# A ten-mixer transformer stack on one core: the last gate blocks of two layers, their value matmuls and the weight splits are placed differently

## The chip, the core and the metric

The kernel runs on one core of a Trainium2 chip. The core's engines are TensorE (PE in the profile; its weight loads are PEld), VectorE (DVE), ScalarE (ACT), GpSimd (POOL) and SyncE (SP); each works through a queue of its own in order, and they wait for each other by semaphores. The metric is device time of one execution in microseconds (us). Three runs of the kernel before are shown: 2591.42, 2593.69 and 2613.07, median 2593.69.

## The reference, cut to what matters

512 tokens of width 1024, all in float32, pass through two stacks. The first has four layers: MLA, SWA (a sliding window), NSA, MLA; each is

```
shift, scale, gate = split(silu(c) @ ada_w[i] + ada_b[i], 3)
h = rmsnorm(x, norm_g[i]) * (1 + scale) + shift
x = x + gate * mixer(h)

swa: q, k, v, g = split(h @ w_in);  q, k = rope(q), rope(k)
     o = softmax over a band of keys, with a sink per head (16 heads, 2 key heads, d = 64)
     return (o * silu(g)) @ w_out
nsa: the same with three branches: compressed keys, selected blocks, a window;
     o = g0*o_c + g1*o_s + g2*o_w;  return (o * silu(g)) @ w_out
```

The second stack has two layers with four mixers each: retention, differential attention, SSD and mLSTM. All attention is causal.

## The kernel before, in words

Activations are kept transposed: a "block" is 128 features by 512 tokens. Every large product is made in three matmuls of split operands (`product`, L514: high x high, high x low, low x high), 128x128 weights against 512 columns. So each 1024x256 unit of weights must be split: DVE copies it rounded into a high part (`part_high`, L1560) and subtracts it for the low part (`part_low`, L1566; in `split` the same at L1537 and L1538). SP loads the units into three slots of `wring`, one after the other; a load waits until the unit three before it is used up. There are two slots for high parts, so a split waits for the unit two before it.

The silu gate of a layer has four such units, ("gate", 0) to ("gate", 3), each two blocks of 8 chunks by 3 matmuls. ACT copies a finished block from PSUM and writes its tanh into one of the two slots `th` (that is `pr[:, 2:4]`); DVE multiplies (`gate`). In the same DVE loop stand `ada_rows`: steps of the next layers' `silu(c) @ ada_w`, 16 per modulation part, whose weights POOL loads (512 KB each, at most two ahead; POOL waits for DVE's rows before it issues the next). PE sums them in `modulation`, 16 one-column matmuls at L613.

Attention (`attention` on PE, ACT and DVE, `normalise` on POOL) goes over steps: one pair of heads by one tile of 128 queries, i.e. 16 steps in MLA and in the later differential attention, 32 in SWA, 64 in NSA. A step: PE scores (L643; in SWA first the sink columns, L636), DVE masks and takes the row max (L1639), ACT exponentiates and sums (L1218), DVE inverts the sum (L1643), POOL scales (L2326), PE transposes (L657) into one of two banks, DVE or ACT copies (L1662, L1665, L1230, L1233), PE multiplies with the values (L822 in SWA, L914 in NSA). Scores run two steps ahead of the transposes, values one behind. The probabilities of step m stand in slot m mod 4 (`rows_slot`); slot 1 is `pr[:, 2:4]`, so ACT's first exp waits for the last gate. When a pair of heads is done, DVE takes it through three stages (`out_unit`: multiply with the gate, high part, low part), one per step. At steps 5 and 9 DVE writes a whole high part of the next weight unit, at steps 7 and 11 its low part. The output projection follows.

What is ahead of the first step: in SWA the four gate units, two modulations and their waits. In NSA also the compressed branch: its scores for four query tiles (L857) lie after gate units 0 (two tiles), 1 and 2; DVE and ACT make a softmax of each, POOL multiplies twice per tile (L2342, L2344; in POOL's queue behind its ada loads), PE transposes after the modulations (L891) and DVE copies (L1960). PSUM: four banks for scores (0 to 3; 0 to 2 are the ring A of the gates, 3 to 5 the ring V), two for transposes (4, 5), two for outputs (6, 7: ring O).

## Time and profile before

| | |
|---|---|
| median of 3 runs | 2593.69 us |
| the profiled execution: time, span | 2609.59 us, 2607.7 us |
| busy: PE, PEld, DVE, ACT, POOL | 91%, 69%, 60%, 29%, 18% |
| mean granted TensorE clock | 0.936 of full |
| chain that ended last | PE 70%, DVE 16%, ACT 5%, issue 3%, DMA 3%, POOL 2% |
| from first to last attention matmul: SWA | 435.2 to 544.7 us |
| the same: NSA | 831.9 to about 993 us |

The page gives busy time per engine, the span in 40 equal slices, the chain of waits that ended last, and groups of instructions. The trace can be asked for stretches ("windows"), for the instructions of one engine in order of time ("timeline"), for waits and for the chain.
### The profile page before, as it was taken

Reading aid. Unit: us, or ns where it says so; the run is one execution under the profiler, and the core shown is the slowest. Engines: PE = TensorE matmul, PEld = TensorE weight load, DVE = VectorE, ACT = ScalarE, POOL = GpSimd, SP = SyncE. Lnnn points to the kernel's source line nnn. Section 1 sums busy time; section 2 is a strip of 40 time slices with the busy share of each in tenths; the row PEclk is TensorE's granted clock in tenths of the full one; section 3 lists DMA queues with packets and bytes.
Section 4 is the critical chain, followed back from the end, with each engine's and each line's share of the span. In section 5 each row is a group of like instructions: output and inputs, shape, how many; then the busy total and the mean of one; then the engine's idle time right before and its main releaser. Section 6 shows DMA issues by size and latency. Waiting matters only on the chain.

```text
span 2607.7 us, 30434 instructions
## 1 busy us (share of the span) xinstructions
PE 2373.2 (91%) x11909; PEld 1790.4 (69%) x11909; DVE 1561.3 (60%) x2556; ACT 754.0 (29%) x1638; POOL 456.6 (18%) x624
## 2 busy tenths in 40 slices
PE   3989899998998999899699989999889998999987
PEld 2767677776776667677577856586667786658666
DVE  7566674564276766557645478664744546866473
ACT  2343212313102561433312152323310225232321
POOL 1212212311013551202100012200320001220030
PEclk6999898588998999999799999999999999999999
DMA  6540465032474004240122211122122221112111
GB/s 222 153 129 8 122 146 130 1 113 81 89 157 102 2 2 113 82 121 1 65 65 65 81 33 49 49 81 65 55 75 81 65 66 33 49 49 81 56 58 64
DMA packets 222544, 199.49 MB, mean 77 GB/s; under 512 B 85859, under 2 KB 205507, under 8 KB 222147
## 3 DMA queue, kind: packets, MB, share of 16 engines
q1 hardware_dynamic: 210883, 155.60, 20.9%
q0 software_dynamic: 11520, 41.95, 5.4%
q8 instruction: 96, 1.57, 0.3%
q14 instruction: 45, 0.37, 0.0%
HBM read 194.39 MB, written 2.10 MB: 75 GB/s over the span
## 4 chain that ended last, share of the span: by engine, by line
PE 70%; DVE 16%; ACT 5%; issue 3%; DMA 3%; POOL 2%; SPq 0%; DVEq 0%; ACTq 0%; POOLq 0%
PE bank L517 15%; PE bank L518 15%; PE bank L519 15%; PE bank L643 5%; PE bank L657 3%; PE bank L679 3%; DMA mix<-in_ada_w 2%; DVE wring_parts L1538 2%; PE bank L593 2%; DVE whi_parts L1537 2%; DVE mix L1727 1%; DVE qb L2060 1%; PE bank L791 1%; DVE bank L1639 1%; PE bank L537 1%
## 5 line engine op out<-in xcount | busy, mean ns | idle before, releaser
L518 PE MATMUL bank<-h_parts,whi_parts 128*128 128x512 f32 (+2 forms) x1248 | 496.9, 398 | 0.0
L1538 DVE TENSOR_TENSOR wring_parts<-wring,whi_parts 128x2048 fp32r<-128x2048 f32 (+1 forms) x126 | 283.6, 2251 | 4.3
L518 PEld LDWEIGHTS bank<-h_parts,whi_parts 128*128 128x128 f32 (+2 forms) x1248 | 231.7, 186 | 64.0 <-issue 5.9
L1537 DVE CAST whi_parts<-wring 128x2048 fp32r<-128x2048 f32 (+1 forms) x126 | 150.7, 1196 | 175.6 <-PE bank L519 142.9
L518 PE MATMUL bank<-mix_parts,whi_parts 128*128 128x512 f32 x512 | 204.5, 399 | 0.0
L517 PE MATMUL bank<-vt_parts,whi_parts 128*128 128x512 f32 (+2 forms) x456 | 191.9, 421 | 5.9 <-DVE wring_parts L1538 5.9
L519 PE MATMUL bank<-vt_parts,wring_parts 128*128 128x512 f32 (+2 forms) x456 | 182.2, 400 | 0.0
L643 PE MATMUL bank<-kb,qb 64*128 64x128 f32 (+3 forms) x1024 | 160.1, 393 | 6.2 <-ACT pr L1175 2.7
L1639 DVE CUSTOM_DVE_ANT_0 bank<-bank,causal 128x256 f32<-128x256 f32 (+3 forms) x256 | 120.5, 513 | 70.8 <-PE bank L643 70.3
L517 PE MATMUL bank<-pt_parts,whi_parts 128*128 128x512 f32 x368 | 151.7, 412 | 10.5 <-ACT kb L1150 5.3
L517 PE MATMUL bank<-mix_parts,whi_parts 128*128 128x512 f32 (+1 forms) x392 | 155.2, 396 | 0.0
L519 PE MATMUL bank<-mix_parts,wring_parts 128*128 128x512 f32 (+1 forms) x392 | 155.0, 396 | 0.0
L2307 POOL DMA_DIRECT2D mix<-in_ada_w x80 | 64.6, 808 | 505.9 <-DVE mix L1727 493.9
L519 PE MATMUL bank<-pt_parts,wring_parts 128*128 128x512 f32 x368 | 146.0, 397 | 0.0
L519 PE MATMUL bank<-whi_parts,h_parts 128*128 128x256 f32 (+1 forms) x480 | 134.0, 279 | 0.0
L643 PEld LDWEIGHTS bank<-kb,qb 64*128 64x128 f32 (+1 forms) x1024 | 102.8, 221 | 33.4 <-issue 18.6
L1727 DVE SCALAR_TENSOR_TENSOR mix<-mix,cond 128x512 f32<-128x512 f32 x140 | 105.2, 752 | 30.4 <-DMA mix<-in_ada_w 26.2
L1606 DVE SCALAR_TENSOR_TENSOR tmp<-bank,st 128x512 f32<-128x512 f32 x55 | 38.0, 692 | 126.6 <-PE bank L593 123.7
L518 PEld LDWEIGHTS bank<-mix_parts,whi_parts 128*128 128x128 f32 x512 | 97.7, 191 | 23.4 <-issue 1.0
L1218 ACT ACTIVATE pr<-bank,stat 128x128 f32<-128x128 f32 (+4 forms) x160 | 72.8, 460 | 133.4 <-DVE stat L1639 102.4
L517 PEld LDWEIGHTS bank<-vt_parts,whi_parts 128*128 128x128 f32 (+2 forms) x456 | 84.8, 186 | 38.0 <-issue 9.2
L517 PE MATMUL bank<-kb_parts,whi_parts 128*128 128x512 f32 x224 | 91.2, 407 | 16.1 <-POOL mix_parts L2370 11.5
(406 smaller groups left out, 5047.8 us busy)
## 6 DMA issues: line engine op xcount, KB each, us to landing
wring<-in_w_in SPq DMA_DIRECT2D x60, 1024.0 KB, 5.2
mix<-in_ada_w POOLq DMA_DIRECT2D x80, 512.0 KB, 4.6
wring<-in_w_out SPq DMA_DIRECT2D x16, 1024.0 KB, 5.3
wring<-in_mla_w_in SPq DMA_DIRECT2D x10, 1024.0 KB, 5.5
wring<-in_mla_w_out SPq DMA_DIRECT2D x8, 1024.0 KB, 5.3
wring<-in_swa_w_in SPq DMA_DIRECT2D x32, 256.0 KB, 4.7
wring<-in_nsa_w_in SPq DMA_DIRECT2D x32, 256.0 KB, 4.5
wring<-in_nsa_w_in SPq DMA_DIRECT2D x6, 1024.0 KB, 5.1
```

The lines of the kernel that those rows point to most:

```text
L517: pe.matmul(bank, lh, rh, start=start, stop=False)
L518: pe.matmul(bank, lh, rl, start=False, stop=False)
L519: return pe.matmul(bank, ll, rh, start=False, stop=stop)
L643: mm = pe.matmul(b[s][:, lo:hi], q[:, i * P:(i + 1) * P], k[:, first + lo:first + hi], start=(c == 0), stop=(c == len(terms) - 1 and (c == ...
L657: mm = pe.transpose(turn_bank(n)[:, at * P:(at + 1) * P], rows_slot(m, s)[:, c * P:(c + 1) * P], ident[:, :])
L679: mm = pe.matmul(bank[:, j * P:], v(j), pt[:, u % 2, j, j * P:], start=(j == 0 and not opened), stop=(j == NT - 1 and last))
L1218: act.activation(rows_slot(m, s)[:, 0:wide], bank[:, 0:wide], ACT.Exp, scale=-1.0, bias=stat_at(0, m, s), accum_out=stat_at(1, m, s)).then ...
L1537: chain(dve.tensor_copy(high, whole))
L1538: dve.tensor_tensor(low, whole, high.bitcast(F32), ALU.subtract).then_inc(done, 1)
L1639: dve.tensor_tensor_reduce(bank, bank, mask, -1.0, least, ALU.add, ALU.min, stat_at(0, m, s)).then_inc(max_ready, 1)
L1727: dve.scalar_tensor_tensor(out=to, in0=t, scalar=cond[:, k:k + 1], in1=to, op0=ALU.mult, op1=ALU.add).then_inc(ada_step, 1)
L2307: pool.dma_start(ada_ring[:, u % 2, :].rearrange("p (k n) -> p k n", k=2), w[:, k:k + 2, c:c + S]).then_inc(ada_loaded[u % 2], 16)
```

## The change

- SWA and NSA: gate unit 3 is not made ahead of attention. `late_gates` on PE makes its two blocks, both at once over the 8 chunks, in four pieces of 12 matmuls: two pieces after score 0, one after score 1, one after the first transposes. They go to ring O. The modulations, and in NSA the transposes of the compressed branch, come after the first two pieces, inside the attention. ACT copies the two blocks and takes the tanh into `vt[:, 0:2, 512:]` after its step 0; DVE multiplies them at steps 2 and 3. DVE's part of the modulations (in NSA also the copies of the transposes) comes after row max 0.
- SWA and NSA: values run two steps behind the transposes; DVE's stages of a finished pair come one step later.
- The `ada_rows` of the eight gates are spread over six: 3, 3, 3, 3, 2, 2.
- NSA: compressed scores of tiles 2 and 3 both follow gate unit 1.
- All six attentions: the weight splits at steps 5 to 11 become pieces, one a step from step 3 to 14: two high pieces of 1024 columns and four low ones of 512 for each of two units.
- `rows_slot`: the slot that shares memory with `th` is now that of step 3, and in SWA and NSA ACT waits for the last early gate before its exps of step 3.

The diff, cut where lines repeat what is said above:

```diff
-PREPARE_AT = (5, 9)
+PREPARE_FROM = 3
 AHEAD = 2
+LATE_VALUES = (1, 2)
 LOW_LAG = 2
...
-NSA_SCORES = ((0, 1), (2,), (3,))
+NSA_SCORES = ((0, 1), (2, 3), ())
...
-            return (pr[:, 0, :], pr[:, 1, :], pr[:, 2, :], pr[:, 3, :], raw[:, 0, 4:], raw[:, 1, 4:], rs[:, :], tmp[:, :])[2 * (m % 4) + s]
+            return (pr[:, 0, :], pr[:, 1, :], raw[:, 0, 4:], raw[:, 1, 4:], rs[:, :], tmp[:, :], pr[:, 2, :], pr[:, 3, :])[2 * (m % 4) + s]
...
+            def late_gates(L):
+
+                slots = by_chunk(weights(L, ("gate", 3)))
+                b = [open_bank(O, (L, "gate", 6 + j)) for j in range(2)]
+                for k in range(KC):
+                    for j in range(2):
+                        mm = product(b[j][:, :], [t[:, k, j * P:(j + 1) * P] for t in slots], hk(k), k == 0, k == KC - 1)
+                        if k == KC - 1:
+                            mm.then_inc(O.full, 1)
+                    if k == KC - 1:
+                        used(O.filled((L, "gate", 7)))
+                    if k % 2:
+                        yield
+
             def in_tokens(L, name, ring, key, n, at=0, slots=None):
...
-            def attention(L, scores, values):
+            def attention(L, scores, values, fill=None):
 
                 todo = steps(L)
+                behind = 2 if L in LATE_VALUES else 1
 
                 def score(m):
...
                     score(m)
+                    if fill:
+                        fill(m)
                 for m in range(len(todo)):
                     if m + AHEAD < len(todo):
                         score(m + AHEAD)
                     turn(m)
-                    if m:
-                        value(m - 1)
-                value(len(todo) - 1)
+                    if fill and m == 0:
+                        fill(AHEAD)
+                    if m >= behind:
+                        value(m - behind)
+                for m in range(len(todo) - behind, len(todo)):
+                    value(m)
...
                     rope_swap((L, "k", 0))
-                    for i in range(4):
+                    for i in range(3):
                         in_blocks(L, ("gate", i), A, [(L, "gate", 2 * i + j) for j in range(2)])
-                    modulations(L)
                     pe.wait_ge(*cnt(rope_done, 9))
-                    pe.wait_ge(*A.emptied((L, "gate", KC - 1)))
-                    pe.wait_ge(*V.emptied(last_modulation(L)))
+                    pe.wait_ge(*A.emptied((L, "gate", 5)))
+                    late = late_gates(L)
+
+                    def fill(at):
+                        next(late)
+                        if at == 0:
+                            next(late)
+                            modulations(L)
+                            pe.wait_ge(*V.emptied(last_modulation(L)))
...
                             mm.then_inc(V.full, 1)
-                    for i in range(4):
+                    for i in range(3):
...
-                        if i < 3:
-                            for t in NSA_SCORES[i]:
-                                compressed_scores(t)
-                    modulations(L)
-                    for i in range(NT):
-                        pe.wait_ge(*cnt(cmp_pool))
-                        bank = open_bank(V, (L, "tc", i))
-                        for g in range(4):
-                            mm = pe.transpose(bank[:, g * P:(g + 1) * P], pc[:, i, g * P:(g + 1) * P], ident[:, :])
-                        mm.then_inc(V.full, 1)
-                    pe.wait_ge(*V.emptied((L, "tc", NT - 1)))
-
-                    pe.wait_ge(*A.emptied((L, "gate", KC - 1)))
+                        for t in NSA_SCORES[i]:
+                            compressed_scores(t)
+                    pe.wait_ge(*A.emptied((L, "gate", 5)))
+                    late = late_gates(L)
+
+                    def fill(at):
+                        next(late)
+                        if at == 0:
+                            next(late)
+                            modulations(L)
+                            for i in range(NT):
+                                pe.wait_ge(*cnt(cmp_pool))
+                                bank = open_bank(V, (L, "tc", i))
+                                for g in range(4):
+                                    mm = pe.transpose(bank[:, g * P:(g + 1) * P], pc[:, i, g * P:(g + 1) * P], ident[:, :])
+                                mm.then_inc(V.full, 1)
...
+            def late_gates(L):
+                for b in range(6, KC):
+                    act.wait_ge(*O.filled((L, "gate", b)))
+                    bank = O.tile((L, "gate", b))
+                    act.activation(mix[:, b, :], bank[:, :], ACT.Copy)
+                    act.activation(vt[:, b - 6, S:], bank[:, :], ACT.Tanh, scale=0.5).then_inc(O.empty, 1)
+
             def attention(L):
                 todo = steps(L)
-                act.wait_ge(*th_read[-1])
+                if L not in (1, 2):
+                    act.wait_ge(*th_read[-1])
 
                 def exps(m):
                     u, i = todo[m]
...
                     exps(m)
                 for m in range(len(todo)):
                     if m + AHEAD < len(todo):
+                        if m == 1 and L in (1, 2):
+                            act.wait_ge(*th_read[-1])
                         exps(m + AHEAD)
                     keep_turned(m)
+                    if m == 0 and L in (1, 2):
+                        late_gates(L)
 
...
+                (_, name), _, part = unit
+                if part is whole:
+                    return lambda slot: slot[:, first:first + n]
+                return lambda slot: part(slot)[:, first // UNIT:(first + n) // UNIT, :]
+
             def part_low(whole, low, high, done):
 
                 dve.wait_ge(*cut[0])
...
 
             prepared = [0]
 
-            def prepare_high():
+            def prepare_piece(piece):
 
                 s = prepared[0]
                 n = split_units[s]
-                dve.wait_ge(w_loaded[n % W_SLOTS], landed[n])
-                if s >= HI_SLOTS:
-                    dve.wait_ge(*unit_done[split_units[s - HI_SLOTS]])
-                part = units[n][2]
-                part_high(part(W[n % W_SLOTS]), part(W_HIGH[s % HI_SLOTS]))
-
-            def prepare_low():
-
-                s = prepared[0]
-                prepared[0] += 1
-                n = split_units[s]
-                part = units[n][2]
-                part_low(part(W[n % W_SLOTS]), part(W_LOW[n % W_SLOTS]), part(W_HIGH[s % HI_SLOTS]), w_split)
+                whole, low, high = W[n % W_SLOTS], W_LOW[n % W_SLOTS], W_HIGH[s % HI_SLOTS]
+                if piece == 0:
+                    dve.wait_ge(w_loaded[n % W_SLOTS], landed[n])
+                    if s >= HI_SLOTS:
+                        dve.wait_ge(*unit_done[split_units[s - HI_SLOTS]])
+                if piece < 2:
+                    part = columns_of(units[n], 1024 * piece, 1024)
+                    part_high(part(whole), part(high))
+                else:
+                    part = columns_of(units[n], 512 * (piece - 2), 512)
+                    dve.wait_ge(*cut[0])
+                    got = dve.tensor_tensor(part(low), part(whole), part(high).bitcast(F32), ALU.subtract)
+                    if piece == 5:
+                        got.then_inc(w_split, 1)
...
-            def attention(L, out_unit):
+            def late_gate(L, b):
+
+                dve.wait_ge(*O.emptied((L, "gate", b)))
+                O.take((L, "gate", b))
+                dve.scalar_tensor_tensor(out=mix[:, b, :], in0=vt[:, b - 6, S:], scalar=1.0, in1=mix[:, b, :],
+                                         op0=ALU.add, op1=ALU.mult).then_inc(late_gated, 1)
...
+                outs = [(u, stage) for u in range(pairs(L)) for stage in range(3)]
                 for m in range(AHEAD):
                     row_max(m)
-                row_sum(0)
+                    if m == 0:
+                        if early:
+                            early()
+                            row_sum(0)
+                if not early:
+                    row_sum(0)
                 if L >= 4:
...
                     keep_turned(m)
-                    stage = m % NT - (0 if L in (0, 3) else 1)
-                    if u and 0 <= stage < 3:
-                        out_unit(u - 1, stage)
-                    if m in PREPARE_AT:
-                        prepare_high()
-                    if m - 2 in PREPARE_AT:
-                        prepare_low()
-                for stage in range(3):
-                    out_unit(pairs(L) - 1, stage)
+                    if early and m in (2, 3):
+                        late_gate(L, 4 + m)
+                    since = m - (0 if L in (0, 3) else 1) - (1 if L in LATE_VALUES else 0)
+                    if since >= NT and since % NT < 3:
+                        out_unit(*outs.pop(0))
+                    if 0 <= m - PREPARE_FROM < 12:
+                        prepare_piece((m - PREPARE_FROM) % 6)
+                for unit_stage in outs:
+                    out_unit(*unit_stage)
 
             def residual(L, b):
...
+                    for b in range(6):
                         gate((L, "gate", b), mix[:, b, :])
-                        ada_rows(2)
+                        ada_rows(3 if b < 4 else 2)
                         if b in (1, 3):
...
-                    for i in range(4):
+                    for i in range(3):
                         for j in range(2):
                             gate((L, "gate", 2 * i + j), mix[:, 2 * i + j, :])
-                            ada_rows(2)
+                            ada_rows(2 if i == 2 else 3)
                         if i < 2:
                             prepare()
                         if i:
                             for t in NSA_SCORES[i - 1]:
                                 compressed_factors(t)
-                        if i < 3:
-                            for t in NSA_SCORES[i]:
-                                compressed_max(t)
-                modulation(L, 2)
-                if L + 1 < len(LAYERS):
-                    modulation(L + 1, 0)
+                        for t in NSA_SCORES[i]:
+                            compressed_max(t)
+
+                def next_modulations():
+                    modulation(L, 2)
+                    if L + 1 < len(LAYERS):
+                        modulation(L + 1, 0)
+                    if L == 2:
+                        for i in range(NT):
+                            dve.wait_ge(*V.filled((L, "tc", i)))
+                            dve.tensor_copy(ex[:, :, i * P:(i + 1) * P], V.take((L, "tc", i))[:, :].rearrange("p (g n) -> p g n", g=4)).then_inc(V.empty, 1)
+
+                if kind == "mla":
+                    next_modulations()
                 if kind == "nsa":
-                    for i in range(NT):
-                        dve.wait_ge(*V.filled((L, "tc", i)))
-                        dve.tensor_copy(ex[:, :, i * P:(i + 1) * P], V.take((L, "tc", i))[:, :].rearrange("p (g n) -> p g n", g=4)).then_inc(V.empty, 1)
...
-                attention(L, out_unit)
+                attention(L, out_unit, next_modulations if kind != "mla" else None)
```

## Rows read from the trace of the kernel before

**Rows 1.** The page: granted TensorE clock in 40 slices, tenths.

```profile
PEclk6999898588998999999799999999999999999999
```

**Rows 2.** Stretches: us, busy PE PEld DVE ACT POOL (instructions), PEclk, DMA share, GB/s.

```profile
433.00:433.50 0.50, 0.50 (x6) 0.50 (x5) 0.00 (x0) 0.00 (x0) 0.17 (x1) 0.79 1.12 188
435.20:544.70 109.50, 109.00 (x688) 80.73 (x688) 57.19 (x201) 38.94 (x144) 33.12 (x64) 0.51 0.03 7
542.00:543.00 1.00, 1.00 (x11) 0.83 (x11) 0.92 (x2) 0.00 (x0) 0.41 (x1) 0.74 0.00 0
```

**Rows 3.** Timeline, PE before SWA attention: start, length, work [idle before <-releaser].

```profile
428.48 1.84 PE L613 MATMUL bank<-ones,mix 128*128 128x1 f32 x16
432.20 2.61 PE L613 MATMUL bank<-ones,mix 128*128 128x1 f32 x16 [1.87 <-DVE mix L1727]
435.22 0.59 PE L636 MATMUL bank<-sink,ones 1*128 1x1 f32 x4 [0.42 <-issue]
```

**Rows 4.** Chain: start, share, line; a gate matmul, then SWA tiles.

```profile
428.17 0.23 PE bank L518
...
451.94 1.16 PE bank L643 x8
...
453.71 1.05 PE bank L822 x8
454.77 0.52 PE bank L636 x4
...
456.44 1.04 PE bank L657 x4
```

**Rows 5.** Chain of work in NSA attention, full clock.

```profile
842.08 0.59 PE bank L914 x8
842.67 0.65 PE bank L643 x8
843.32 1.03 PE bank L657 x8
```

**Rows 6.** Timeline of PE between NSA gates and attention.

```profile
815.78 1.84 PE L613 MATMUL bank<-ones,mix 128*128 128x1 f32 x16
819.50 3.57 PE L613 MATMUL bank<-ones,mix 128*128 128x1 f32 x16 [1.88 <-DVE mix L1727]
...
831.90 1.65 PE L643 MATMUL bank<-kb,qb 64*128 64x128 f32 x12 [0.78 <-DVE ex L1960]
```

**Rows 7.** Timeline of POOL, same stretch.

```profile
819.75 0.72 POOL L2307 DMA_DIRECT2D mix<-in_ada_w  x1 [4.00 <-DVE mix L1727]
...
828.90 1.05 POOL L2344 TENSOR_TENSOR kb<-kb,aux 128x512 f32<-128x512 f32 x1
```

**Rows 8.** Timeline of DVE before SWA attention: last gate block.

```profile
429.88 0.69 DVE L1619 SCALAR_TENSOR_TENSOR mix<-pr,mix 128x512 f32<-128x512 f32 x1 [3.29 <-ACT pr L1175]
```

**Rows 9.** Stretches of differential attention, as Rows 2.

```profile
1495.00:1532.00 37.00, 27.65 (x214) 20.67 (x213) 29.45 (x103) 22.91 (x79) 9.72 (x16) 1.00 0.08 28
2148.00:2156.00 8.00, 7.78 (x43) 5.92 (x41) 3.86 (x15) 4.03 (x13) 1.19 (x3) 0.65 0.00 0
```

**Rows 10.** NSA attention without its first 8 us, as Rows 2.

```profile
840.00:994.00 154.00, 144.71 (x1411) 102.12 (x1408) 105.08 (x375) 90.27 (x291) 79.46 (x122) 1.00 0.01 2
```

**Rows 11.** Chain of work: compressed scores of two query tiles.

```profile
774.50 3.53 PE bank L857 x32
```

**Rows 12.** Timeline of DVE in NSA attention: two low parts.

```profile
853.63 2.29 DVE L1566 TENSOR_TENSOR wring_parts<-wring,whi_parts 128x2048 fp32r<-128x2048 f32 x1
...
864.60 0.69 DVE L1566 TENSOR_TENSOR mix_parts<-mix,qb_parts 128x512 fp32r<-128x512 f32 x1
```

**Rows 13.** Timeline of POOL, same stretch.

```profile
842.87 0.88 POOL L2326 TENSOR_SCALAR pr<-pr,stat,gbr 128x128 f32<-128x128 f32 x2 [0.36 <-DVE stat L1643]
...
853.25 4.07 POOL L2326 TENSOR_SCALAR pr<-pr,stat,gbr 128x128 f32<-128x128 f32 x4
```

**Rows 14.** Waits of PE in NSA attention: total us, times, longest.

```profile
PE bank L657 <- POOL tmp L2326: 6.0, 11, 1.3
```

16 lines of the change are left out of this document (10 added, 6 removed).

## The prediction

> **What bounds the kernel now.** I read the page first. TensorE (PE) is busy for 91% of the span, so a gain must come from PE work that gets shorter or from PE's idle time. The row of granted clocks [rows 1] then shows where PE is slow: most slices have 8 or 9 tenths, one has 5. Stretches of that region (the windows view) show that the clock falls from 2.4 to 1.2 GHz near 433.3 us and comes back near 542.5 us, which is SWA attention from its first matmul to the output projection: 109.5 us at a mean clock of 0.51, PE busy 109.0 of them [rows 2]. There PE waits for nobody; it is at half clock. It went down after a thin stretch: the last dense gate matmul ended near 428.5, then came 16 one-column matmuls (L613), 1.87 us idle, 16 more, and the first scores at 435.22 [rows 3].
>
> Next the price of a tile of 128 queries with two key tiles. In SWA at half clock (chain of waits): sinks 0.52, scores 1.16, transposes 1.04, values 1.05, so 3.77 us [rows 4]. The same matmul shapes in NSA attention at full clock: scores 0.65, values 0.59, four transposes half of 1.03, so 0.52 [rows 5]. The sinks have no row at full clock; half of 0.52 and 0.52 bound them and I take 0.35, since a tiny matmul is more overhead than columns. Warm tile: 2.11 us. A step with one key tile has half of each part but the sinks: 0.88 + 0.35 = 1.23.
>
> The second loss is ahead of NSA attention: last gate matmul near 815.8, first score at 831.90 [rows 6]. In between PE has only 32 one-column matmuls and 16 transposes; it waits for POOL, whose queue holds an ada weight load behind DVE's last ada row (4.00 us) and whose compressed factors come only after it, until 829.95 [rows 7].
>
> **The change part by part.** The sum is made against the profiled execution (span 2607.7 us, 2609.6 with what lies around it); that one is 0.6% above the median of the runs shown, 2593.7, and the difference carries over unchanged.
>
> (1) SWA attention's clock. Gate unit 3 (48 dense matmuls at 0.23 us [rows 4], 11.1 us) leaves the front and comes in four pieces of 12: two after score 0, one after score 1, one after turn 0. The modulations (about 1.84 us each [rows 3]) stand behind the first two pieces. After unit 2 PE waits for its last gate (copy, tanh: 1.2 us or so, since DVE starts behind both at 429.88 [rows 8] where PE ended near 428.6). The thin stretch is then two modulations, a short drain of V and score 1, some 5 us; before it was about as long when the clock fell. So I expect a dip as well, but now 24 dense matmuls follow it, and near 542.5 us the clock came back when only transposes and values were left, without sinks and scores [rows 2]: it does not take much.
>
> Whether it then holds is the whole question. For it: the differential attention, made of the same kind of small matmuls, held 1.00 for 37 us with PE busy only 27.65 of them, 214 matmuls recorded; and its twin in the next layer came back from 1.2 GHz with 43 matmuls in 8 us, inside attention work [rows 9]. SWA at 1.2 GHz put 688 in 109.5 us [rows 2], 6.3 per us, with narrow operands; warm, the same work is passed 1.8 times as fast (3.77 by 2.11). I expect two stable states, and the change puts the stage into the upper one. The Trainium skill, "TensorE: Matmul & The Clock Gate", section "Why this matters for your kernels", says that keeping TensorE busy brings the full clock and that the loss comes from idle gaps. The first half disagrees with the trace here: busy 109.0 of 109.5 us did not bring it [rows 2]; by it SWA would already be warm, parts (3) and (4) alone would be left, and the time would be 2588; the row leaves that no chance. The second half, which no row tests for this stage, would keep the clock up.
>
> Warm PE work: 8 groups of (1.23 + 3 x 2.11) = 60.5 us. DVE is now near: it is busy 57.19 in this stage [rows 2], plus some 1.3 for split pieces and 1.4 for two late gates (0.69 each [rows 8]), so 59.9. Two in-order engines that both need 60 do not overlap perfectly. Were PE as full as in NSA attention (94%, 144.71 of 154 [rows 10]), 64 us; were DVE only as full as in the differential one (29.45 of 37, 80% [rows 9]), 75. PE and DVE lie between, I take 71. Gain 109.5 - 71 = 38.5, between 34 and 45 by these two.
>
> (2) Entry to SWA. Before: unit 2 ended near 428.5 - 11.1 = 417.4, attention began 435.2: 17.8 us. After: wait 1.2, gates 11.1, modulations 3.7, drain 0.5, one piece at half clock + 2.8, and up to 1 where exps(3) stands behind ACT's four late gate activations and POOL and PE wait for it: 20.3. Cost 2.5. Without the dip it gains 0.3; with two pieces slow it costs 5.3. The ada rows now run three per gate over six gates instead of two over eight, so their loads come a third denser. A late row stalls DVE, but 5.5 us of gate matmuls lie between it and the modulation, where before PE stood idle 1.87 [rows 3]; I take 0, and at most those 1.87. The second part of the thin stretch, DVE's first row max, is followed by its wait for the modulations; row_sum 0, row max 1, ACT's exps 1 and POOL queue behind it, and the next piece (2.8 us) hides that.
>
> (3) NSA entry. Scores 2 and 3 follow gate unit 1, so their factors are started before the last gates end; the last ada row falls with gate 5, and so does POOL's queued load. Walking the engines: unit 1 ended near 815.8 less two units (22.2) and two score tiles (half of 3.53 each [rows 11]), so 790.1. Unit 2's second block then needs a bank that is free only after DVE has done a gate, three ada rows, a weight split, two factors and a max, by my estimate 12 us, and ACT its exp: 802.9, which is a new wait of some 3.5 us for PE. That block is 5.6 long, gate 5 ends at 808.5, DVE's last ada row at 811.8; POOL's load (0.72) and four factors took 10.2 from 819.75 [rows 7], so they end at 822 instead of 830. Under them lie score 0, 24 gate matmuls and the modulations. Score 1 starts near 823.3, 6 us ahead with half a gate unit still to be slotted in at latencies that the first tiles have anyway. I get 6 with a warm clock and 2 with a dip, take 4; ends -2 (dip and late ACT) and 8.
>
> (4) Split pieces and later values. A low part over 2048 columns takes 2.29, over 512 it takes 0.69 [rows 12], so four pieces cost 2.8; the high part in halves about 0.2 more. Per split +0.7 of DVE, hidden in MLA and NSA by PE, half exposed in differential attention. For it: while the 2.29 runs, POOL's four normalisations take 4.07 where two took 0.88 [rows 13], and PE waits on POOL's tmp 6.0 us in NSA, 11 times [rows 14]. The Trainium skill, "SBUF — State Buffer", section "SBUF: two separate sides", calls the port pair of VectorE and GpSimd a lock held for a whole instruction; the trace agrees. By that rule a piece blocks at most 0.69 us instead of 2.29, some 1.6 for each of 12 splits where POOL is late. I take 2 in all, -1 to 5. Values two behind remove waits on copies of the turned rows, 0.2 us in NSA; nothing by themselves, and they keep SWA from stalling at full clock. Out stages move one step later; one stage more (0.7) is left behind the loop, under the first chunks of the output projection. The new row slots only free exps(0) to exps(2) from the last tanh: counted in (2).
>
> Sum: 38.5 - 2.5 + 4 + 2 = 42. Profiled 2567.6, median 2551.7; **forecast 2552 us**. Its own range: least 34 - 5.3 - 2 - 1 = 26, most 45 + 0.3 + 8 + 5 = 58, so 2536 to 2568.
>
> **The rivals.** *The clock stays at 1.2 GHz in SWA.* For it: nothing in the stage raised it for 108 us [rows 2], and the thin stretch is not shorter. Against: 24 dense matmuls after it. Then (1) is 0, (2) costs 5 to 6, (3) and (4) give 4 and 2: 2594, within 2586 to 2600. This is also the case in which the change does not do what it could.
>
> *It rises and falls again midway.* One long wait, on split pieces or out stages of a DVE that is 85% full, would be enough, and nothing later brings it back. Each of 32 tiles that stays cold costs about 1.2 us: half of them give 2552 + 20 = 2572; with three quarters cold 2581.
>
> *Slower: NSA attention loses its clock.* Its entry becomes thin (factors, transposes) and is cut by pieces, as SWA's was. The place is PE in the 162 us from 831.9; price: 144.7 us of PE work times 0.79 (3.77 by 2.11) = 114, so 2666 if all of it stays cold, and slower by 1% from 60% on. Against: before, it came back in the first tiles and was 1.00 from 840 us on [rows 10].
>
> *DVE is slower than I think.* With DVE full only 75%, SWA needs 80 us: 2561; inside the forecast's range.
>
> **How the numbers follow.** Forecast (warm SWA) 0.62, midway 0.10, cold 0.22, slower 0.06. A measurement of this kernel tells about 1% (26 us) from no change. Faster by over 1%: nearly all of the first, under half of the second, 0.63. Within 1%: 0.31. Slower: 0.06. The range for 8 in 10: the warm case without its ends (0.58), midway (0.10) and half of the cold one (0.12) give 2537 to 2594.
>
> **What would show it.** Right: in SWA attention PEclk at 1.00, its stage near 71 us, score rows of 0.65 and value rows of 0.59 instead of 1.16 and 1.05; DVE busy about 85%. POOL's factors before 825 in NSA. L1566 low parts of 0.69 only, and the 4.07 of POOL gone. Wrong: a 5 in the clock row at SWA, with PE again busy all the time; or NSA's first 20 us at 0.50.

## The result, and the profile after

Median 2567.30 us (2566.33 to 2568.20, 4 runs) against 2592.62 us before (2591.42 to 2613.07, 4 runs, the three shown and one more beside it). The medians differ by 25.3 us. The ratio is 0.9895, 95% interval 0.9847 to 0.9943; it and the ratios below are those on record, not quotients of the medians. They leave out as slow each run that took over 1.5% longer than the fastest of its kernel: two in e4, and one in each set of the kernel before that stands beside the experiments. The profiled execution of the changed kernel took 2567.36 us (span 2565.4), which is at its median; that of the kernel before, 2609.59. Between the two profiles lie 42.2 us, the sum that was forecast, and between the medians 25.3. Most of this section is about that difference of 17.

The row of granted clocks, to be read beside [rows 1]: the 5 at SWA is gone.

```profile
PEclk7989899989999998999899999999999999999998
```

Stretches of the changed kernel (us, busy PE PEld DVE ACT POOL, PEclk, DMA share, GB/s): SWA from score 1 to the output projection, the same without its dip, and NSA attention from score 1 to its last score. They answer to [rows 2, 10].

```profile
431.46:504.36 72.90, 69.68 (x705) 52.68 (x705) 56.78 (x207) 40.20 (x144) 34.66 (x64) 0.98 0.09 16
436.00:504.36 68.36, 65.14 (x685) 49.01 (x684) 55.64 (x201) 39.17 (x140) 32.70 (x60) 1.00 0.09 17
795.95:945.60 149.65, 144.98 (x1387) 103.41 (x1388) 107.18 (x392) 92.32 (x297) 75.54 (x124) 1.00 0.04 9
```

From 436 us on SWA is at full clock. DVE is busy 55.64 of 68.36 us there, 81%. The timeline of PE on the way in (start, length, work, idle before and releaser) answers to [rows 3]:

```profile
421.18 0.38 PE L652 MATMUL bank<-sink,ones 1*128 1x1 f32 x4 [1.22 <-issue]
...
427.57 3.63 PE L628 MATMUL bank<-ones,mix 128*128 128x1 f32 x32
...
431.46 0.38 PE L652 MATMUL bank<-sink,ones 1*128 1x1 f32 x4 [0.26 <-DVE mod L1770]
...
434.00 0.63 PE L519 MATMUL bank<-h_parts,whi_parts 128*128 128x512 f32 x1
...
442.92 0.49 PE L659 MATMUL bank<-kb,qb 64*128 64x128 f32 x4
...
504.36 0.50 PE L518 MATMUL bank<-qb_parts,whi_parts 128*128 128x512 f32 x1
```

PE waits 1.22 us (the profile says "issue"; by the code it is the last early gate), makes score 0, two pieces and both modulations; then the clock does fall, as a dense matmul of 0.63 us instead of 0.40 at 434.00 shows, and the third piece ends at full clock again. The output projection begins at 504.36, before at 544.7.

The front of NSA, DVE, PE and POOL in one timeline, answers to [rows 6, 7]:

```profile
744.17 1.54 DVE L1793 SCALAR_TENSOR_TENSOR mix<-mix,cond 128x512 f32<-128x512 f32 x2 [2.84 <-DMA mix<-in_ada_w]
...
752.07 0.79 PE L518 MATMUL bank<-pt_parts,whi_parts 128*128 128x512 f32 x1 [4.75 <-ACT kb L1399]
...
773.01 0.50 PE L518 MATMUL bank<-pt_parts,whi_parts 128*128 128x512 f32 x1 [3.72 <-ACT kb L1399]
...
784.19 0.72 POOL L2378 DMA_DIRECT2D mix<-in_ada_w  x1 [4.88 <-DVE mix L1793]
...
793.38 1.05 POOL L2415 TENSOR_TENSOR kb<-kb,aux 128x512 f32<-128x512 f32 x1
...
795.95 0.71 PE L659 MATMUL bank<-kb,qb 64*128 64x128 f32 x8 [0.79 <-DVE ex L2027]
```

PE waits twice for a bank whose compressed scores ACT has not yet exponentiated (L1399). The first time DVE was late because its ada weights were (2.84 us). POOL's four factors still end at 794.4, and score 1 starts at 795.95. The waits of PE in NSA attention are down from those of [rows 14]; the columns are total us, times, longest:

```profile
PE bank L673 <- POOL pr L2397: 4.0, 7, 1.3
PE bank L673 <- DVE pt L1722: 0.5, 1, 0.5
```

Where the 42.2 us between the profiles lie, with two later profiles beside them (us). Each stretch runs from one matmul with the rope's `swap` matrix (`rope_swap`) to another, the same ones in every kernel, so a layer's stretch takes in the norm and the first projections of the next one:

| stretch | before | before, again (e1) | after | after, again (e12) |
|---|---|---|---|---|
| start to the key swap of SWA | 383.2 | 386.1 | 385.6 | 385.0 |
| from there to the first swap of NSA | 261.4 | 234.7 | 221.2 | 218.3 |
| NSA layer, to the first swap of layer 3 | 450.2 | 453.2 | 449.4 | 449.2 |
| MLA layer, to the first swap of the second stack | 214.6 | 214.8 | 211.9 | 214.7 |
| second stack | 1298.3 | 1300.9 | 1297.3 | 1294.7 |

Nearly the whole effect is in the SWA layer: 40.2 of 42.2 us. The NSA layer, for which the forecast had some 5 us, gives 0.8. The other stretches scatter by 3 to 6 us from profile to profile; where it was read, the granted clock goes with it (the MLA layer took 211.9 us at a mean clock of 0.94 and 214.6 to 214.8 at 0.93). And the kernel before is not one kernel in time: its own SWA layer differs by 27 us between two profiles.

### The profile page after: what moved, and what is told of

It reads as the page before. It is cut to its first block, busy times and chain, and to the rows that moved or that the text cites. A ratio compares the mean times of both kernels' runs of the same rounds, so it can differ in the third digit from the quotient of the medians.

```text
span 2565.4 us, 30479 instructions
## 1 busy us (share of the span) xinstructions
PE 2328.1 (91%) x11909; PEld 1759.8 (69%) x11909; DVE 1563.0 (61%) x2604; ACT 753.7 (29%) x1638; POOL 453.4 (18%) x624
## 4 chain that ended last, share of the span: by engine, by line
PE 68%; DVE 17%; ACT 5%; DMA 3%; issue 3%; POOL 3%; SPq 0%; DVEq 0%; ACTq 0%; POOLq 0%
PE bank L518 15%; PE bank L519 15%; PE bank L520 15%; PE bank L659 4%; DMA mix<-in_ada_w 3%; PE bank L700 3%; PE bank L673 2%; DVE wring_parts L1581 2%; PE bank L608 2%; DVE mix L1793 2%; DVE whi_parts L1580 2%; DVE qb L2131 1%; PE bank L812 1%; PE bank L945 1%; DVE bank L1699 1%
## 5 line engine op out<-in xcount | busy, mean ns | idle before, releaser
L518 PE MATMUL bank<-pt_parts,whi_parts 128*128 128x512 f32 x368 | 155.6, 423 | 17.2 <-ACT kb L1399 8.5
L659 PE MATMUL bank<-kb,qb 64*128 64x128 f32 (+3 forms) x1024 | 142.2, 351 | 6.8 <-ACT pr L1206 3.9
L659 PEld LDWEIGHTS bank<-kb,qb 64*128 64x128 f32 (+1 forms) x1024 | 89.7, 189 | 34.0 <-issue 20.4
L518 PE MATMUL bank<-qb_parts,whi_parts 128*128 128x512 f32 x256 | 105.1, 410 | 0.0
```

What stands on the lines that cost most here:

```text
L518: pe.matmul(bank, lh, rh, start=start, stop=False)
L659: mm = pe.matmul(b[s][:, lo:hi], q[:, i * P:(i + 1) * P], k[:, first + lo:first + hi], start=(c == 0), stop=(c == len(terms) - 1 and (c == ...
```

## The experiments

**The spread of before (e1).** The kernel before, unchanged, three rounds.

> The kernel before, unchanged, looked at once more: its profiled execution took 2609.6 us, the other runs shown 2591 to 2594 and 2613. Theory A (the 18 us sit in one stage: in the shorter executions part of SWA attention runs at full clock): a look of about 2592 us shows SWA attention in some 91 us instead of 109.5. Theory B (they sit in many short dips of the clock elsewhere): SWA attention takes 109 us in every look, and the sum of the other stages is 18 us shorter.

2593.5 us median, 2587.4 to 2612.0 in 10 runs; the profiled execution took 2591.5. With the 78 runs made beside the experiments there are 88 of this kernel: 24 lie between 2609 and 2620 us, 64 between 2576 and 2603. The mean granted clock parts them in the same way: 0.931 to 0.937 in the 24 (the profile of before has 0.936), 0.942 to 0.952 in the 64. The stretches of SWA attention in the profile of 2591.5 us:

```profile
438.00:452.00 14.00, 13.61 (x86) 10.46 (x87) 6.12 (x28) 5.18 (x21) 5.03 (x10) 0.50 0.19 47
454.00:464.00 10.00, 9.87 (x110) 7.40 (x110) 8.70 (x26) 4.86 (x18) 3.87 (x8) 1.00 0.01 2
464.00:466.00 2.00, 0.78 (x13) 0.58 (x11) 1.87 (x7) 0.72 (x3) 1.10 (x2) 1.00 0.00 0
468.00:486.00 18.00, 18.00 (x113) 13.50 (x114) 11.71 (x38) 6.22 (x24) 6.15 (x12) 0.50 0.01 1
488.00:514.00 26.00, 26.00 (x288) 19.71 (x290) 20.06 (x80) 15.43 (x58) 13.15 (x26) 1.00 0.01 2
```

The clock fell at 437, came back near 453.8, fell again near 467.7 and came back for good near 487.9. In the profile of before it stayed down until 542.5 [rows 2]. So theory A holds (its SWA attention, scores from 438.1 to 514.4, ends 24.9 us earlier than before's 539.3). What happened just before it fell at 467 is in the timeline of DVE, POOL and PE:

```profile
462.39 2.28 DVE L1566 TENSOR_TENSOR wring_parts<-wring,whi_parts 128x2048 fp32r<-128x2048 f32 x1
...
464.59 0.15 DVE L1643 RECIPROCAL stat<-stat 128x2 f32<-128x2 f32 x1
...
464.84 1.10 POOL L2326 TENSOR_SCALAR pr<-pr,stat,ones 128x256 f32<-128x256 f32 x2 [2.91 <-DVE stat L1643]
...
465.99 0.66 PE L657 MATMUL bank<-ident,pr 128*128 128x128 f32 x4 [1.22 <-POOL pr L2326]
```

DVE's whole low part (2.28 us) holds the reciprocal of the row sum, POOL waits 2.91 us for it, PE 1.22 for POOL; PE was busy 0.78 of 2 us, and the clock fell behind it. That the stall is the cause rests on e3 and e9 below, where the same happens, and on e4; it was not forced by an edit of its own.

**Each part alone (e2, e3, e4).** The kernel before with one part of the change.

```diff
 e2  LATE_VALUES = (1,)   late gates, ada rows, row slots: SWA only; splits whole
 e3  LATE_VALUES = (2,)   the same for NSA only, with its order of scores; splits whole
 e4  -PREPARE_AT = (5, 9)   nothing else
     +PREPARE_FROM = 3
```

> The change in SWA alone: late gate pieces, ada rows in six gates, values two behind, new row slots; NSA and the weight splits as before. Main theory (nearly the whole gain is SWA's clock): SWA attention from its first regular scores to the output projection 73 us at a clock near 1, total 2568 to 2572 us. Rival (the change in NSA and the split pieces carry a third of the gain): 2576 to 2582 us. Rival (the smaller pieces of DVE work are needed for PE to stay at full clock): the clock falls again within SWA, total above 2585.

2572.2 us (2570.7 to 2580.0 in 10 runs), ratio 0.9896 (0.9861 to 0.9930). Its profile (2579.9 us) from 444 us on:

```profile
444.00:501.00 57.00, 53.69 (x584) 40.41 (x582) 49.14 (x176) 33.45 (x125) 30.14 (x54) 1.00 0.10 20
```

SWA is at full clock in spite of whole splits, so the main theory holds, with the median at the upper end of its 2568 to 2572. The four edits within it (pieces, ada rows, later values, row slots) are parted only by e5 and e10; ada rows and row slots have no run of their own.

> The change in NSA alone. From the two profiles: the front of NSA lost 6 us (two waits of 4.75 and 3.72 us for a bank and two dips of the clock), its attention gained 10, so 4 us net: theory: its total is 4 us below the kernel before in the same state, 2588, and SWA attention stays at half clock. Rival (the gain of NSA attention came from split pieces and not from the late values): 0 to +6 us, 2592 to 2598.

2590.6 us (2574.8 to 2612.9), ratio 0.9982 (0.9940 to 1.0024): no difference that can be told from the spread of before. SWA is untouched here, and its profile shows the same fall as e1, behind the same kind of stretch:

```profile
466.00:468.00 2.00, 1.12 (x12) 0.79 (x12) 1.54 (x9) 1.08 (x5) 1.33 (x3) 1.00 0.00 0
470.00:516.00 46.00, 46.00 (x292) 33.97 (x288) 24.89 (x90) 16.74 (x63) 14.46 (x29) 0.50 0.01 1
```

Its NSA attention took 151.8 us (scores from 819.3 to 971.1, 5.6 of gate pieces within) against 153.7 before, but its front lost as much: the NSA layer took 449.6 us against 450.2. The 4 us of my theory are not there.

> The split pieces alone, in all six attentions; gates, values and row slots as before. My prediction had 2 us of gain for it (-1 to 5). Theory: 2590 us, PE waits for POOL in NSA attention down from 5.9 to about 4 us. Rival (the gain in NSA attention is all theirs): 6 us or more, 2586. Rival (more DVE instructions delay it): 2594 or more.

2574.4 us, ratio 0.9897 (0.9864 to 0.9931): 8 of 10 runs between 2569.6 and 2580.3, two at 2611.5 and 2613.7. None of the three expectations had this size. SWA attention in its profile (2569.8 us):

```profile
436.00:452.00 16.00, 15.62 (x100) 11.80 (x100) 7.52 (x33) 6.54 (x26) 5.04 (x11) 0.50 0.20 45
454.00:500.00 46.00, 45.10 (x488) 33.97 (x486) 41.09 (x154) 27.36 (x103) 23.56 (x46) 1.00 0.01 2
```

The entry is cold as before. But once the clock is back, near 452, it stays: DVE is as full, in pieces of 0.7 us, and PE is busy 45.10 of 46 us. NSA attention took 153.7 us, as before, and PE waited 5.3 us in it for POOL, against 5.0 before: the pieces alone give it nothing. What they gave is SWA's clock.

**What decides at the entry (e5, e6, e9).** e5 moves two of the four pieces of the changed kernel; e6 makes the kernel before enter attention straight from dense work; e9 adds dense work to the kernel before.

```diff
 e5   def fill(at):                      (SWA)
-         next(late)
          if at == 0:
-             next(late)
+             for _ in range(4): next(late)
              modulations(L)
 e6   for i in range(4):                 (before, SWA; ada rows 3, 3, 3, 3, 2, 2)
+         if i == 3: modulations(L)
          in_blocks(L, ("gate", i), ...)
-     modulations(L)
 e9  +def dense():                       (before, SWA; after score 1 and after turn 0)
+        for k in range(12): pe.matmul(spare_bank, h_parts[:, k % KC, 0:P], h_parts[:, k % KC, :])
```

> The changed kernel, but in SWA all four pieces of gate unit 3 stand after score 0 and ahead of the modulations, so that nothing dense follows the thin stretch. Theory (the 24 dense matmuls after the modulations are what makes attention start at full clock): SWA starts at 1.2 GHz again; as the split pieces are in, the clock comes back some 17 us later in most runs, as in the run with the pieces alone: 2572 to 2580 us, with single runs at 2600 or more. Rival (the later values or the shorter thin stretch hold the clock up anyway): within 1 us of 2567.

2604.0 us, 2601.5 to 2606.4 in 10 runs, ratio to before 1.0041 (1.0011 to 1.0071). The modulations' stretch, then attention:

```profile
430.00:434.00 4.00, 3.81 (x34) 3.67 (x32) 0.32 (x3) 0.00 (x0) 0.00 (x0) 1.00 0.56 130
436.00:536.00 100.00, 100.00 (x624) 73.98 (x622) 54.59 (x199) 38.22 (x141) 31.17 (x60) 0.50 0.01 3
```

The first half of the theory is shown, and larger than I had it: two pieces, 24 matmuls, stand one place earlier, and the kernel is 37 to 40 us slower than the changed one (2567.3, and 2563.6 in e12). PE is busy 100.00 of 100.00 us at half clock. Its second half fell: in the profile the clock did not come back after 17 us, and the mean clock of all ten runs, 0.935 to 0.938, is that of executions which are cold through SWA.

> The kernel before with one edit, in SWA: the 16 ada rows are spread over the first six gates and the two modulations stand ahead of gate unit 3, so that 48 dense matmuls lie between them and attention. No late gates, values one behind, whole splits. Theory (what counts is to enter attention from dense work): it starts at full clock, total 2570 to 2576 us. Rival (whole splits stall PE at full clock and throw it back, as at 465 us in the repeated look at the kernel before): starts at full clock and falls after step 9: 2582 to 2595. Rival (the wait for the last gate drops the clock by itself): as before, 2594.

2616.8 us, 2588.7 to 2625.0, nine of ten above 2612; ratio 1.0073 (1.0033 to 1.0112). Dense work, the first tiles, the rest:

```profile
430.00:438.00 8.00, 8.00 (x35) 6.48 (x34) 0.69 (x1) 1.09 (x2) 0.00 (x0) 0.98 0.00 0
438.00:444.00 6.00, 3.98 (x38) 2.91 (x36) 2.52 (x12) 2.91 (x10) 0.70 (x2) 1.00 0.58 124
444.00:542.00 98.00, 97.78 (x608) 72.23 (x608) 51.98 (x183) 34.94 (x130) 30.29 (x60) 0.50 0.02 4
```

My theory fell. Attention was entered at full clock from eight dense us, and the clock fell within its first tiles: PE waits 1.22 us for the last gate, 0.65 for the first exp, 0.38 for POOL, and was busy 3.98 of 6 us. The entry has two thin places, the modulations and the latency of the first tiles, and e6 mended one. That mending the other as well would have been enough was not run.

> The kernel before with work added and nothing else: in SWA 12 dense matmuls (128x128 by 512 columns, 2.8 us each dozen) whose result nobody reads stand behind score 1 and 12 more behind the first transposes, where the changed kernel has the last two pieces of its late gates. Theory (what brings and holds the full clock is dense work between the first tiles): SWA attention runs at full clock although 5.6 us of work are added; with whole splits it can fall once midway: median 2575 to 2585 us, none of the runs above 2600. Rival (the pieces help because they take work out of the front, or the later values and row slots do it): the clock stays down as often as before, median 2594 to 2600, single runs near 2618.

2604.2 us (2599.7 to 2615.4), ratio 1.0041 (1.0010 to 1.0071). Four stretches of its profile:

```profile
434.00:442.00 8.00, 7.58 (x39) 6.66 (x39) 1.97 (x11) 1.83 (x8) 0.92 (x3) 0.50 0.64 139
444.00:474.00 30.00, 28.33 (x283) 21.11 (x283) 22.22 (x75) 14.54 (x54) 11.34 (x22) 1.00 0.01 2
474.00:478.00 4.00, 2.79 (x32) 2.07 (x30) 3.26 (x11) 1.02 (x5) 1.53 (x3) 0.97 0.01 2
478.00:534.00 56.00, 56.00 (x348) 41.27 (x350) 27.03 (x105) 20.89 (x77) 18.00 (x36) 0.50 0.00 1
```

The size was missed: I had 2575 to 2585 and no run above 2600, and nine of ten were above. The mechanism is half right. The clock is down at 434 to 442 and comes up inside the first dense dozen, 8 to 10 us earlier than in e1 and e4, where nothing dense stood there; attention then runs at 1.00 for 33 us. At 474 PE stalls beside the second whole split (2.79 of 4 us busy), the clock falls, and stays down for 56 us; beside the first one, at 463, it did not fall. In this profile 5.6 us were added and the clock was won and lost: dense work lifts it, and does not keep it.

**What holds it (e7, e10).** The changed kernel with whole splits; with the values one step behind.

```diff
 e7  -PREPARE_FROM = 3
     +PREPARE_AT = (5, 9)
 e10 -LATE_VALUES = (1, 2)
     +LATE_VALUES = ()
```

> The changed kernel with whole weight splits at steps 5 to 11 again, all else as changed. Theory (pieces matter only where the clock has fallen; with a warm entry they save 1 to 3 us of waits): 2568 to 2571 us. Rival (they carry the gain of NSA attention too): 2574 or more.

2571.0 us, ratio 0.9930 (0.9889 to 0.9971): 8 of 10 runs from 2566.4 to 2575.5, two at 2594.1 and 2595.7. The profile (2570.8 us), SWA and NSA attention:

```profile
436.00:499.50 63.50, 60.23 (x635) 45.51 (x634) 51.68 (x185) 37.02 (x134) 31.04 (x56) 1.00 0.10 18
793.60:945.30 151.70, 146.99 (x1387) 104.75 (x1388) 106.38 (x384) 92.20 (x297) 76.20 (x124) 0.99 0.04 8
```

The eight runs fit the theory within some us. The other two are as slow as before's middle and have no profile of their own; their mean clock was 0.943, against 0.952 to 0.956 in the eight, so they lost clock somewhere. That a whole split threw them back, as in e1 and e9, is likely but not shown. NSA attention costs 2.1 us more than after's 149.65, but not for want of pieces. It was entered at half clock here and at full clock in the changed kernel (this run's row, then after's):

```profile
793.60:797.00 3.40, 3.38 (x13) 2.75 (x14) 1.07 (x6) 1.02 (x4) 1.15 (x3) 0.50 0.00 0
795.95:799.35 3.40, 3.40 (x20) 2.70 (x20) 1.06 (x6) 1.02 (x4) 1.68 (x4) 1.00 0.00 0
```

Over its first 11.4 us the mean clock was 0.83, which costs some 1.9 us, and PE waited for POOL 4.0 us in the stage, in both kernels. So here too the pieces give NSA nothing that can be seen. The entry is cold in e8 as well, with pieces in, and in e3; why, no run shows.

> The changed kernel with the values of SWA and NSA one step behind the transposes, as before, and the out stages back with them. Theory (the later values are worth the short waits on copies): 2568 to 2571 us, SWA at full clock. Rival (they keep SWA from stalling when it is at full clock): runs at 2590 appear.

2571.9 us, 2568.2 to 2573.4 in 9 runs, ratio 0.9914 (0.9886 to 0.9941), no run near 2590. SWA keeps its clock; the cost is in NSA attention, 155.6 us:

```profile
795.10:950.70 155.60, 147.69 (x1403) 104.15 (x1403) 107.24 (x392) 92.34 (x297) 79.76 (x125) 1.00 0.04 8
```

That is 5.95 us more than with later values, out of 8.3 us between its median and e12's. PE waits for POOL 6.3 us in it, against 4.0, and for DVE's copies 1.2 against 0.5. These 3.0 us are half of it; the other half is in no wait, and up to the output projection PE is busy 153.30 us against 151.06 with the same matmuls. It stays unexplained.

**The front of NSA, and a version that beats both (e8, e11, e12).**

```diff
 e8   gate(L, 2 * i + j)
+     if j: compressed_max of the unit's tiles      (was behind rows, split and factors)
-     ada_rows(3, 3, 3, 3, 2, 2)
+     ada_rows(2, 2, 3, 3, 3, 3)
 e11 as e8, and:
+     compressed_factors(0), (1) ahead of the split; (2), (3) ahead of the last rows
+     ada_rows(2, 3, 3, 4, 2, 2)
+     POOL: the four factors ahead of its last two ada loads of the stage
+     PE: late gate piece 0 ahead of score 0, in SWA and NSA
```

> The changed kernel with another order of DVE in the front of NSA: the maxima of the compressed scores come right behind the second gate of the unit, ahead of its ada rows and the weight split, and the ada rows run 2, 2, 3, 3, 3, 3 over the six gates instead of 3, 3, 3, 3, 2, 2. It aims at the two waits of PE for a bank (4.75 and 3.72 us) and the dips of the clock behind them (1.6 to 2.4 us each). Theory: most of it comes back, total 2556 to 2561 us. Rival (DVE is the bound of that stretch, the waits only move): 2564 to 2567. Rival (the last ada row comes later and the modulations wait for it): above 2568.

2563.1 us (2560.8 to 2564.1, 4 runs), ratio 0.9886 (0.9816 to 0.9957). By its total it is not told from the changed kernel, which had 2567.3 and 2563.6 us in its two sets of runs; the profile says more. Both bank waits are gone, and something new is late (DVE, then PE):

```profile
772.79 1.54 DVE L1811 SCALAR_TENSOR_TENSOR mix<-mix,cond 128x512 f32<-128x512 f32 x2 [4.42 <-DMA mix<-in_ada_w]
...
784.88 1.11 PE L929 MATMUL bank<-ident,kb 128*128 128x128 f32 x4 [1.24 <-POOL kb L2440]
...
786.78 1.23 PE L661 MATMUL bank<-kb,qb 64*128 64x128 f32 x8 [0.78 <-DVE ex L2052]
```

The last ada rows waited 4.42 us for their weights, POOL's factors queued behind that load, and PE waited 5.2 us for them in four parts. The waits moved, as the second rival has it, though not all of them. Gates and NSA attention together took 4.8 us less than in the changed kernel (from the last swap matmul, 722.2 to 937.9 against 725.1 to 945.6).

> A version meant to beat both. The changed kernel with three more edits: in the front of NSA DVE takes the maxima of the compressed scores ahead of the ada rows and the factors of tiles 0 and 1 ahead of the weight split, those of 2 and 3 ahead of the last ada rows (rows 2, 3, 3, 4, 2, 2); POOL multiplies the factors ahead of its last two ada loads; in SWA and NSA the first late gate piece stands ahead of score 0 and covers the wait of 1.2 us for the last early gate. Theory: 6 us less than the 2563 us of the version with the maxima first, since PE's 5.2 us of waits for POOL go, and 1 to 2 us for the pieces: 2553 to 2558. Rival (the queue of DVE is full there, the waits move to the gates): 2560 to 2564. Rival (with one piece less between score 0 and the modulations SWA loses its clock): above 2590.

2559.0 us, 2556.4 to 2560.0 in 6 runs, ratio to before 0.9860 (0.9822 to 0.9898). Beside it on the same chip:

> The changed kernel once more, beside the others on one chip. Theory: 2567 us within 2, with none of the spread of the kernel before (2577 to 2620). Rival (its four runs were lucky): single runs above 2580.

2563.6 us, 2563.0 to 2569.2 in 6 runs, ratio 0.9883 (0.9844 to 0.9921). I had 2567 within 2, so two sets of runs of one kernel can lie 3.7 us apart; the small differences of e7 and e8 to the changed kernel, which did not run beside it, are no larger. e11 did run beside it. The two sets do not overlap; e11 is 4.6 us faster than the changed kernel, 1 us short of my range. PE in its NSA front:

```profile
766.87 0.80 PE L520 MATMUL bank<-pt_parts,whi_parts 128*128 128x512 f32 x1 [3.21 <-DVE wring_parts L1592]
...
780.67 3.31 PE L926 MATMUL bank<-ident,kb 128*128 128x128 f32 x16
...
784.85 0.71 PE L661 MATMUL bank<-kb,qb 64*128 64x128 f32 x8 [0.88 <-DVE ex L2048]
```

The transposes of the compressed branch now run without a break, and score 1 starts 63.6 us after the last swap matmul (784.85 against 721.26) where the changed kernel takes 70.8. A wait of 3.21 us for the weight split that was put behind the factors is what it pays. Its SWA layer took 218.2 us, e12's 218.3: the earlier piece gave nothing there.

## Why the prediction was right, and where it was not

**The sum.** The median came out at 2567.3 us where 2552 was forecast, 0.7 us inside the upper end of the range. The direction and the main mechanism were right: SWA attention went from half to full clock. The size at the median was 25.3 us instead of 42. Against the profiled execution the sum was 42 and the profiles differ by 42.2, and that agreement is luck: the terms are off by +4.8, +1.9, -9.9 and +7.7 us, and 4.3 were lost outside them. Term by term, from the profiles:

| step | forecast | measured |
|---|---|---|
| (1) SWA attention's clock | 38.5 (34 to 45) | 43.3 |
| (2) entry to SWA | -2.5 | -0.6 |
| (3) entry to NSA | +4 (-2 to 8) | -5.9 |
| (4) pieces, later values | +2 (-1 to 5) | 9.7 in NSA attention |

(1) and (2): from the end of gate unit 2 to the output projection before took 127.3 us, after 84.6 (419.8 to 504.4). In it are 1.4 for the last gate, 13.2 for 48 gate matmuls and 3.9 for the modulations and their drain, some 18.4 in all; 66.2 us are left for attention. I had 71, because I put PE and DVE halfway between two stages with more waits; the stage is nearer its PE work of 60.5 (DVE is at 81%, forecast about 85). The warm prices were nearly right: scores 0.65, values 0.59, transposes 0.59 (forecast 0.52), sinks 0.31 from start to start (0.35).

(3) has the wrong sign. The new wait in unit 2's second block was forecast at 3.5 us and measured 3.72. The same wait one unit earlier, 4.75 us, was not seen, nor the dips of the clock behind both (0.50 over 752 to 757, 0.66 over 773 to 778, by my estimate 2.5 and 1.7 us). Together they make 9.2 of the 9.9 us. The step that failed is "I take 0" for the denser ada loads: I asked only whether PE's modulation would wait for a late row, and in NSA the compressed maxima stand behind those rows in DVE's queue. e8 bears it out: with the maxima ahead both waits are gone, though it also moved ada rows, so the two were not parted.

(4) The mis-sized term is the later values, "nothing by themselves". By e10 they are worth 5.95 us in NSA attention. I had counted only the waits on copies, and misread those: 0.2 us stands beside POOL's raw, and the row of the copies is

```profile
PE bank L657 <- DVE pt L1662: 1.6, 8, 0.3
```

Nor had I seen that values put between the transposes and the next scores give POOL time (PE's waits for it fall from 6.3 to 4.0 us). Another 3.7 come without them (153.7 against e10's 155.6 less 5.6 of gates), and the clock of the first tiles accounts for it: the first 8 us before ran at 0.50 and 0.57, by my estimate 3.8 us lost, and e10 has 1.00 there. Both together are the 9.7. For the pieces, to which I gave the 2 us, nothing is left in NSA (e4, e7): their low parts take 0.69 us as forecast, and POOL's longest run of four normalisations went from 4.49 to 3.31 us, but PE waits for POOL no less. Their use is in SWA (e4), which the forecast did not have.

The four terms measured add up to 46.5. Of that 2.4 us were lost ahead of SWA, 2.5 between its attention and the first swap of NSA, 1.6 in the projections that open NSA and 1.4 behind its attention, and 3.7 won in layer 3 and the second stack; each is of the size of the scatter in the table.

**The step that failed** is the one ahead of the sum: "the difference carries over unchanged". The profiled execution of before was the case of 24 in 88, cold through the whole of SWA. In the other 64 the higher mean clock, and e1's profile of one of them, say that the clock comes back for a part of it, and those runs had already a good part of the gain. The changed kernel has no such spread (10 runs, 2563.0 to 2569.2). So the change is worth 45 us against the first kind and 25 to 30 at the median. A spread of 22 us in three runs was on the table, and a profile above the median by 16; the 2613.07 among the runs should have been read as a second course of the same program.

**The rivals.** "Midway", which I gave 0.10 for the changed kernel, is what the kernel before does: in e1, in e3 (SWA as before) and in e9 (before with work added) the clock falls behind a stall beside a whole split. Its 2572 us lie nearer to the measured 2567.3 than the forecast's 2552, but the changed kernel did not take that course: its SWA was at 1.00. My clause "nothing later brings it back" fell: it came back after 20 us in e1 and after 48 in e3. "Two stable states" is too strong for the same reason. The cold rival did not come; e5 shows that it hung on where two pieces stand. The slower one, NSA losing its clock, did not come either: its attention was at 1.00.

**The rule.** By the sentence cited from the Trainium skill, "TensorE: Matmul & The Clock Gate", section "Why this matters for your kernels", that a busy TensorE brings the full clock, e5 would have been at full clock after its entry; the rows show 100.00 us busy and 0.50. The half about idle gaps agrees with e1, e6 and e9, and not with e2, where PE stood idle 1.67 of 4 us and the clock stayed. The same page of the Trainium skill, section "Part 1: The HAM clock gate", says that the moment at which the clock first changes varies from run to run, by about half a microsecond either way. The runs agree that it varies, and not in the size: within one program the clock came back in SWA attention after 17 us in one profile and after 109 in another, and the 88 runs lie 43 us apart.

**What stays open.** Why the clock comes back after 17 us in e1, after 16 in e4 and after 109 in the profile of before; why pieces helped in 8 of 10 runs of e4 and in none of e5; why e2's stalls and e7's whole splits left the clock up; why NSA attention is entered cold in some kernels and warm in others. A probe of the entry in steps of a few matmuls would be next.

## What to carry to other kernels

A stage of small matmuls can run at either clock with TensorE busy all the time; look at the granted clock beside busy time, and put dense work that is due anyway between the first tiles, behind the last thin stretch. Then look for the longest instruction of any engine that feeds such a stage and try it in pieces: a stall stood before the clock's fall in e1, e3 and e9, for 20 to 56 us, and the pieces kept the clock up in 8 of e4's 10 runs. And where the runs of a kernel spread, its one profile is one of several courses: take another, and hold its time against the other runs, before a difference is summed on it.

## What the hardware showed that was not expected

- The same program: SWA attention at half clock for 109 us in one execution and for about 37 in another.
- 24 matmuls of 0.23 us, moved by one place, changed a stage from 1.00 to 0.50 for 100 us (e5).
- Matmuls added for nothing raised the clock (e9: from 0.50 before 442 us to 1.00 from 444 on, inside the first dozen).
- A stall need not cost the clock: e2's whole splits left PE busy 1.06 and 1.27 of 2 us at 459 to 463, and it stayed at 1.00; 1.12 of 2 in e3 lost it.
